# Feed-forward in-projections by seven block products in place of eight

## The reference, cut to what matters

```python
D_MODEL = 1024
D_FF = 2816
def swiglu(h, w_in_ff, w_out_ff):
    gu = h @ w_in_ff
    g, u = gu[..., :D_FF], gu[..., D_FF:]
    return (jax.nn.silu(g) * u) @ w_out_ff
def _ffn_sublayer(x, mod, j, nw_pre, nw_post, w_in_ff, w_out_ff):
    shift, scale, gate = _mod(mod, j)
    y = swiglu(_pre(x, nw_pre, shift, scale), w_in_ff, w_out_ff)
    return x + FFN_RES * gate * rmsnorm(y, nw_post)
```

## Time and profile before

| | us |
|---|---|
| median of 3 runs | 2815.43 |
| lowest, highest | 2812.68, 2815.85 |
| the profiled execution | 2815.84 |
| its span in the trace | 2814.1 |
| PE busy | 2647.8 (94%) |
| DVE busy | 1363.8 (48%) |
| ACT busy | 865.3 (31%) |
| POOL busy | 114.6 (4%) |

### The profile page before, as it was taken

The page is one execution under the profiler, slowest core; times in us unless marked ns, Lnnn a source line. Parts: engine busy times, 40 slices in busy tenths (PEclk is TensorE's granted clock), DMA queues, the critical chain, the costliest instruction groups (busy, mean ns, idle before and its releaser), DMA issues.

```text
span 2814.1 us, 33945 instructions
## 1 busy us (share of the span) xinstructions
PE 2647.8 (94%) x13880; PEld 2376.4 (84%) x13880; DVE 1363.8 (48%) x1871; ACT 865.3 (31%) x1145; POOL 114.6 (4%) x92
## 2 busy tenths in 40 slices
PE   5999999998977989999999999999998878799998
PEld 1999998887966789999988999999887656688887
DVE  2455456655455654544565533334455655522233
ACT  3211113443422451111344411113443433422232
POOL 0000000101200110000010100000101101000001
PEclk9999999999989999999999999999999999899999
DMA  6333334432200233333343333333432201322332
GB/s 228 128 119 120 140 135 164 152 119 79 79 1 1 97 121 120 119 136 140 135 164 123 125 125 137 126 127 120 135 120 80 79 1 60 135 90 97 106 111 75
DMA packets 84735, 314.25 MB, mean 112 GB/s; under 512 B 6944, under 2 KB 23328, under 8 KB 70944
## 3 DMA queue, kind: packets, MB, share of 16 engines
q1 hardware_dynamic: 77360, 297.20, 29.6%
q10 hardware_dynamic: 7280, 15.73, 1.7%
HBM read 310.81 MB, written 2.10 MB: 111 GB/s over the span
## 4 chain that ended last, share of the span: by engine, by line
PE 87%; DVE 7%; ACT 2%; issue 2%; DMA 1%; POOL 0%; SPq 0%; POOLq 0%; DVEq 0%; ACTq 0%
PE ps L1580 47%; PE ps L1594 25%; PE ps L795 5%; DVE w_lo L1319 2%; PE ps L1643 1%; PE ps L1653 1%; PE ps L885 1%; PE ps L901 1%; ACT w_hi L1104 1%; PE ps L876 1%; DVE arena L567 1%; PE ps L894 1%; PE ps L1627 1%; PE ps L895 1%; PE ps L822 1%
## 5 line engine op out<-in xcount | busy, mean ns | idle before, releaser
L1580 PE MATMUL ps<-xn_hi,w_hi 128*128 128x384 f32 (+2 forms) x2528 | 721.9, 340 | 21.8 <-DVE arena L1402 16.8
L1580 PE MATMUL ps<-xn_lo,w_hi 128*128 128x384 f32 (+2 forms) x2528 | 720.5, 340 | 0.0
L1580 PE MATMUL ps<-xn_hi,w_lo 128*128 128x384 f32 (+2 forms) x2528 | 720.3, 340 | 0.0
L1319 DVE TENSOR_TENSOR w_lo<-raw,w_hi 128x2048 fp32r<-128x2048 f32 x211 | 500.2, 2371 | 386.8 <-ACT w_hi L1104 386.6
L1580 PEld LDWEIGHTS ps<-xn_hi,w_hi 128*128 128x128 f32 x2528 | 464.7, 189 | 33.9 <-issue 17.3
L1104 ACT ACTIVATE w_hi<-raw 128x2048 fp32r<-128x2048 f32 x211 | 400.6, 1899 | 266.5 <-PE ps L1594 227.1
L1580 PEld LDWEIGHTS ps<-xn_lo,w_hi 128*128 128x128 f32 x2528 | 464.9, 189 | 11.1
L1580 PEld LDWEIGHTS ps<-xn_hi,w_lo 128*128 128x128 f32 x2528 | 464.5, 189 | 11.3
L1213 ACT ACTIVATE arena<-ps 128x384 f32 (+3 forms) x158 | 72.9, 497 | 1052.4 <-PE ps L1580 1052.4
L1338 DVE SCALAR_TENSOR_TENSOR junk<-acc,silu_row 128x1024 bf16<-128x1024 f32 x224 | 274.0, 1223 | 196.7 <-DMA acc<-w_ada_t 193.3
L1594 PE MATMUL ps<-w_hi,hj_hi 128*128 128x512 f32 x952 | 299.0, 395 | 23.1 <-DVE hj_lo L1327 10.2
(11 more groups left out here) (194 smaller groups left out, 2040.3 us busy)
## 6 DMA issues: line engine op xcount, KB each, us to landing
raw<-w_ff_in SPq DMA_DIRECT2D x104, 1024.0 KB, 5.4
raw<-w_ff_out SPq DMA_DIRECT2D x77, 1024.0 KB, 4.9
acc<-w_ada_t SPq DMA_DIRECT2D x128, 512.0 KB, 3.3
raw<-w_out SPq DMA_DIRECT2D x16, 1024.0 KB, 4.9
raw<-w_in SPq DMA_DIRECT2D x12, 1024.0 KB, 5.2
arena<-w_ada SPq DMA_DIRECT2D x4, 2048.0 KB, 18.7
gate_row<-norm_w ACTq DMA_DIRECT2D x12, 512.0 KB, 4.3
x<-x_in ACTq DMA_DIRECT2D x6, 512.0 KB, 6.8
```

The lines of the kernel that those rows point to most:

```text
L1319: nc.vector.tensor_tensor(w_lo[par][:, 0:width], raw[par][:, 0:width], w_hi[par][:, 0:width].bitcast(F32), ALU.subtract).then_inc(S["w_lo" ...
L1580: ins = mm(ps[:, 4 * b + part + c, col:col + wd], w[:, k, c, :], xx[:, k, t0:t0 + wd], start=(k == 0 and i == 0), stop=(k == KC - 1 and i ...
```

## The change

In stages (0,0), (0,2) and (1,0) the 18 full slots are computed by a form of Strassen's scheme. The left operand is the weights, cut in four: gate or up, and first or second half of the channels (a11, a12 gate, a21, a22 up, 512 columns each). The right one is x, cut by channel half and by token group. The slot's product of 2 x 2 blocks then takes seven block products of 12 matmuls (`product`, `fast_slot`). For it:

- the order of slots becomes lead, tail, then the 18 slots (also in the final stage, which is otherwise as before);
- the sums of x blocks (t) are made once a stage: POOL adds hi and lo of the first group again (`rebuild`, two ops of 1536 columns), DVE does six sums and four lo parts (`t_add`, `t_lo`, 1536 columns each), ACT four hi parts (`t_hi`). Two of the results lie where x does (`t13`), so x is stored to DRAM first in (0,2) and (1,0), and loaded again (from there, or from the input in (0,0)) at the start of the out-projection, six transfers of 512 KB each way;
- POOL makes the sums of weight blocks, four ops of 512 columns a slot (`sums`);
- splits of the weights are by pairs of blocks, 1024, 1024, 1024 and 512 columns (`pair_hi` on ACT, `pair_lo` on DVE), each when the products before have used the old ones;
- three products accumulate onto one already in a bank, after ACT has copied it out (`copy_out`, semaphore snap); DVE combines copies and banks (c11, c22, c12), and c22 must have read bank a before the seventh product goes to it;
- silu now runs on the copies, and DVE does two multiplies a slot;
- `gate_row` is scratch in these slots, so its load (`load_constants`) comes behind the last multiply;
- units go with all 18 slots in the three stages, none with the tail; (0,0) has twelve units in its out slots in place of eight.

The left-out new functions are short: `pair_hi`, `pair_lo`, `t_hi`, `t_add`, `t_lo`, `copy_out` are one instruction each with one wait before it, and ACT's part of the tail is its old part with `pair_hi` and `t_hi` between.

```diff
-ADA_TAIL = {(0, 0): (0, 13)}
-ADA_OUT = {(0, 0): (0, 14), (0, 2): (1, 7)}
+ADA_OUT = {(0, 0): (0, 13, 3), (0, 2): (1, 7, 2)}
 LEAD = 4
+ST = FC - LEAD
...
+        t13 = inner.enter_context(nc.sbuf_tensor("t13", [P, 2, 2, KC // 2, GW], F32R))
...
+        def pair_at(par0, i):
+            off = (0, 2 * HB, 0, 2 * HB)[i]
+            n = HB if i == 3 else 2 * HB
+            return [w_all[:, par0 if i < 2 else 1 - par0, a, off:off + n] for a in range(2)]
...
+        def fast_banks(s):
+            return (0, 1, 2) if s == 0 else (7, 5, 6)
...
+        def tail_steps(sub):
+            for k in range(LEAD, 2 * LEAD):
+                yield k, sub["slot"] + k, k - LEAD, k % 2
...
+        def fast_steps(sub, loop, per):
+            done = 0
+            for a, (l, h0, count) in enumerate(sub["ada_in"]):
+                last = a == len(sub["ada_in"]) - 1
+                trips = count - 1 if last else count
+                if trips:
+                    with loop(trips, per) as i:
+                        for s in range(2):
+                            yield i * 2 + (done + s), s, (l, i, h0, l * HALVES + h0)
+                done += 2 * trips
+            for s in range(2):
+                yield done + s, s, (l, count - 1, h0, l * HALVES + h0)
...
-                    load(n0 + LEAD, (par0 + LEAD) % 2, w_ff_in[l, j // 2, LEAD])
+                    due = {2 * LEAD + 2 * i + s: half for i, half in enumerate(halves) for s in range(2)}
+                    load(n0 + LEAD, (par0 + LEAD) % 2, w_ff_in[l, j // 2, 0])
                     for k in ahead:
                         if k + 1 in ahead:
-                            load(n0 + k + 1, (par0 + k + 1) % 2, w_ff_in[l, j // 2, (k + 1) % FC])
+                            load(n0 + k + 1, (par0 + k + 1) % 2, w_ff_in[l, j // 2, k + 1 - LEAD])
+                        if k == LEAD and sub["fast"] and sub["st"]:
+                            sp.wait_ge(S["xs"], sub["xn"])
+                            for t in range(NT):
+                                sp.dma_start(x_out[t], x[:, t, :]).then_inc(S["xs_out"], 16)
                         if k in due:
                             hl, h = due[k]
-                            for u in (2 * (k % 2), 2 * (k % 2) + 1) if k < FC else (k - FC,):
...
+                        if sub["fast"] and g == 0 and isinstance(s, int) and s == 1:
+                            sp.wait_ge(S["prod"], 6 * ST * (sub["st"] + 1) - 1)
+                            if sub["st"]:
+                                sp.wait_ge(S["xs_out"], 16 * NT * sub["st"])
+                            for t in range(NT):
+                                sp.dma_start(x[:, t, :], (x_out if sub["st"] else x_in)[t]).then_inc(S["x_back"], 16)
...
+            def rebuild(sub):
+                pool.wait_ge(S["xn_done"], sub["xn"])
+                for kh in range(2):
+                    hi, lo = x_block(kh, 0)
+                    nc.gpsimd.tensor_tensor(t_raw(kh), hi.bitcast(F32), lo.bitcast(F32), ALU.add).then_inc(S["t_x"], 1)
+            def sums(sub, q, par, first=False, second=False):
+                n, tq = q + (sub["slot"] + 2 * LEAD), q + ST * sub["st"]
+                a11, a12, a21, a22 = (raw[par][:, i * HB:(i + 1) * HB] for i in range(4))
+                s21 = s_sum(sub["slot"] % 2, first)
+                pool.wait_ge(S[f"w_raw{par}"], n * 8 + (16 - 8 * par))
+                if second:
+                    pool.wait_ge(S["w_used"], 2 * (sub["slot"] + 2 * LEAD) + START)
+                elif not first:
+                    pool.wait_ge(S["q_lo"], tq * 3 - 1)
+                adds.link(nc.gpsimd.tensor_tensor(s21[:, 1, :], a21, a22, ALU.add))
+                adds.mark(nc.gpsimd.tensor_tensor(a21, a11, a21, ALU.subtract))
+                nc.gpsimd.tensor_tensor(s21[:, 0, :], s21[:, 1, :], a11, ALU.subtract).then_inc(S["s_sum"], 1)
+                pool.wait_ge(S["s_sum"], tq * 2 + 1)
+                pool.wait_ge(S["q_lo"], tq * 3 + 1)
+                nc.gpsimd.tensor_tensor(a12, a12, s21[:, 0, :], ALU.subtract).then_inc(S["s_sum"], 1)
...
+                for q, s, half in fast_steps(sub, loop, 0):
+                    tq, n = q + st, q + n1
+                    a, d, b = fast_banks(s)
+                    r = (par0 + s + 1) % 2
+                    last = isinstance(q, int) and q == ST - 1
+                    act.wait_ge(S["prod"], tq * 6 + 1)
+                    copy_out(fast_tmp(2 * s), a)
+                    if not last:
+                        act.wait_ge(S[f"w_raw{r}"], (n + 1) * 8 + (16 - 8 * r))
+                        act.wait_ge(S["prod"], tq * 6 + 2)
+                        pair_hi(sub, 0, r)
+                    act.wait_ge(S["prod"], tq * 6 + 3)
+                    copy_out(fast_tmp(2 * s + 1), a)
+                    act.wait_ge(S["h_done"], n - n0 + sub["proj"])
+                    act.wait_ge(S["prod"], tq * 6 + 4)
+                    copy_out(p5, b)
+                    if not last:
+                        act.wait_ge(S["s_sum"], tq * 2 + 3)
+                        pair_hi(sub, 1, r)
+                    else:
+                        split_w(n + 1, par0)
+                    act.wait_ge(S["c11"], tq + 1)
+                    nc.scalar.activation(fast_tmp(2 * s), fast_tmp(2 * s), ACT.Silu).then_inc(S["silu11"], 1)
+                    act.wait_ge(S["prod"], tq * 6 + 6)
+                    if not last:
+                        act.wait_ge(S["s_sum"], tq * 2 + 4)
+                        pair_hi(sub, 2, r)
+                    else:
+                        first_out(sub)
+                    act.wait_ge(S["c12"], tq + 1)
+                    nc.scalar.activation(fast_tmp(2 * s + 1), fast_tmp(2 * s + 1), ACT.Silu).then_inc(S["silu"], 1)
+                    if not last:
+                        act.wait_ge(S["w_used"], n * 2 + 2 + START)
+                        pair_hi(sub, 3, r)
...
+                        if sub["fast"] and g == 0 and isinstance(s, int) and s == 0:
+                            act.wait_ge(S["h_done"], sub["proj"] + sub["in_slots"])
+                            load_constants(sub)
...
+                for k, n, f, s in tail_steps(sub):
+                    if k < 2 * LEAD - 1:
+                        split_w(n + 1, (par0 + s + 1) % 2)
+                    else:
+                        pair_lo(sub, 0, 0, par0)
+                        pair_lo(sub, 0, 1, par0, first=True)
+                    if k == LEAD:
+                        dve.wait_ge(S["t_x"], 2 * sub["st"] + 1)
+                        t_add(sub, 3, 0, t_raw(2), t_raw(0), ALU.subtract)
+                        t_add(sub, 4, 2, t_raw(3), t_raw(2), ALU.subtract)
+                    if k == LEAD + 1:
+                        dve.wait_ge(S["t_x"], 2 * sub["st"] + 2)
+                        t_add(sub, 5, 3, t_raw(3), t_raw(0), ALU.subtract)
+                        t_add(sub, 6, 1, t_raw(1), t_raw(3), ALU.subtract)
+                    if k == LEAD + 2:
+                        t_lo(sub, 2, 1)
+                    gate_mul(sub, k, f, s, (1,))
+                    if k == LEAD + 2:
+                        t_lo(sub, 1, 2)
+                    if k == LEAD + 3:
+                        t_lo(sub, 3, 3)
+                pair_lo(sub, 0, 2, par0)
+                pair_lo(sub, 0, 3, par0)
+                t_lo(sub, 4, 4)
+                for q, s, half in fast_steps(sub, own.loop, 0):
+                    tq, f, n = q + st, q + LEAD, q + n1
+                    a, d, b = fast_banks(s)
+                    r = (par0 + s + 1) % 2
+                    last = isinstance(q, int) and q == ST - 1
+                    hl, i, h0, g0 = half
+                    g_h, u_h = fast_tmp(2 * s), fast_tmp(2 * s + 1)
+                    dve.wait_ge(S["snap"], tq * 3 + 1)
+                    dve.wait_ge(S["prod"], tq * 6 + 2)
+                    nc.vector.tensor_tensor(g_h, g_h, ps[:, d, 0:GW], ALU.add).then_inc(S["c11"], 1)
+                    if not last:
+                        pair_lo(sub, q + 1, 0, r)
+                    unit(i + g0, i * 4 + (4 * g0 - 16 + 2 * s), 2 * s, streams(hl, h0))
+                    dve.wait_ge(S["snap"], tq * 3 + 3)
+                    dve.wait_ge(S["prod"], tq * 6 + 5)
+                    nc.vector.tensor_tensor(p5, p5, ps[:, a, 0:GW], ALU.add).then_inc(S["c22"], 1)
+                    if not last:
+                        pair_lo(sub, q + 1, 1, r)
+                    else:
+                        split_w(n + 1, par0)
+                    dve.wait_ge(S["prod"], tq * 6 + 6)
+                    nc.vector.tensor_tensor(u_h, u_h, ps[:, b, 0:GW], ALU.add).then_inc(S["c12"], 1)
+                    if not last:
+                        pair_lo(sub, q + 1, 2, r)
+                    else:
+                        first_out(sub)
+                    unit(i + g0, i * 4 + (4 * g0 - 15 + 2 * s), 2 * s + 1, streams(hl, h0))
+                    if s == 1:
+                        finish_units(i + g0, i + h0, i * 4 + (4 * g0 - 12))
```

(46 more changed lines are left out.)

205 lines of the change are left out of this document (148 added, 57 removed).

## The result

The changed kernel takes 2745.97 us (median of 4 runs, 2744.21 to 2750.59), the kernel before 2814.28 in the same comparison: a ratio of 0.976, 95% interval 0.9744 to 0.9775. The forecast was 2783; the gain is 68 us where 32.8 were forecast. On two other chips, where the kernel before took 2812.9 and 2815.2, the same kernel took 2761.4 and 2760.5, ratios of 0.9815 (0.9801 to 0.9828) and 0.9808 (0.9792 to 0.9824). So the gain is 68 us in the first comparison and 51 to 55 in two later ones, and both need a reason. (The chip of the first comparison is not known, and none of the later ones was measured twice, so what I put down to the chip could also be the occasion.)

The account below looks back on a forecast made before the run. TensorE, busy 94%, bounds the kernel before; in the new two-stream slots VectorE would. Gains 28.1 + 32.6, less 7.0, 19.9 and 1.0 (last stage's slot order), give 32.8 us off 2815.84: 2783 us, range 2734 to 2828.

Parts of the forecast that it names:

- The two-stream slot, walked: Slots whose units have two streams: VectorE, held up by GpSimd's sums, sets 15.9 us; 38 slots gain 28.1 us.
- What it removes: 54 in-projection slots: seven products of 12 matmuls for eight, 2.08 us less each, 14.56 left; ceiling 112.3 us.
- One-stream slots: 16 third-stage slots whose units have one stream: TensorE sets the pace at 14.6 us, gaining 32.6 us.
- The start: Start of each of three stages: first new slot's c22 comes late, 2.3 us each, 7.0 lost in all (0 to 18).
- The handover: Products to out-projection: TensorE idles for late out-weights, then runs at half clock; 19.9 us lost in all (0 to 28).
- Costed at nothing: Saving and reloading x, load_constants and the first stage's four extra units hide behind other work: 0 us.
- Free sums: Rival: GpSimd's sums fall into VectorE's waits and beside combines, all slots 14.6 us; 2733 us, chance 0.23.
- Lock without overlap: Rival: every GpSimd sum holds VectorE up in full, two-stream slots 17.0 us; 2824 us, chance 0.19.
- Clock: Rival: TensorE's clock falls after its idle time in each of 38 slots, 2.8 us each; 2889 us, chance 0.05.

Follow-up runs that it names:

- few sums: Changed kernel with a slot's four weight sums made over 8 of 512 columns from each stage's second slot on: 2718.39 us.
- the narrow stream: Changed kernel with the second stream of each modulation unit summed over 64 of its 1024 columns: 2713.64 us.
- the sums on VectorE: Changed kernel with the four weight sums of each slot from the second on made by VectorE, not GpSimd: 2729.29 us beside 2761.42 unedited.
- six sums: Changed kernel with the first and third weight sum of each slot made twice over: 2819.12 us.
- the early load: Changed kernel with the first out-projection weights' load issued ahead of the last slot's two units, not behind: 2742.36 us beside 2761.42 unedited.
- x not saved, first run: Changed kernel without the saves of x, which is reloaded from the input in all three stages; first of two runs: 2760.32 us.

## Why the prediction was right or wrong

**What fell: the size of one term, the two-stream slot.** The step *The two-stream slot, walked* said 15.9 us; it is 15.2 in the first comparison and 15.5 to 15.6 in the two later ones. So the gain on these slots, put at 28.1 us, was about 54 in the first comparison. The 2746 us lie inside the range of 2734 to 2828, but below the 2765 to 2800 that I thought likeliest. The mechanism is the one that it named: few sums, the narrow stream and the sums on VectorE each bring the pitch down to TensorE's or within 0.14 of it, and six sums raise it to 17.1. Three of its parts were too dear. It charged 1.26 us for each of four sums and let 1.0 us of them lie beside other work, 4.05 a slot; measured are 3.6 to 3.8. It took VectorE's own work at 11.4; by the same slot's records it is about 11.2. And it rounded the walk's 15.74 up for hops, which the slot in order of time does not show. Together that is 0.7 us a slot, about 25 us over 38 slots.

**The account of the rest**, from the profiled executions (2815.84 and 2745.93: 69.9 us). From the first new slot's start to the end of its last product the stages take 275.8, 276.8 and 264.3 us; the forecast was 288.5, 288.5 and 267.7. That is 27.8 us better, the slots' 25 among them. The handovers cost 8.7, 8.3 and 3.3 (the wait and the slow matmuls behind it) in place of 9.8, 9.8 and 7.4: 6.7 better. With the 32.8 of the forecast that gives 67.3, and 2.6 us are not placed.

- *What it removes*: right. 648 matmuls, and 14.56 us a slot wherever TensorE sets the pace.
- *One-stream slots*: right, 14.6 forecast, 14.56 measured.
- *The start*: near. The first c22 of each stage is about 3.0 us late where 2.3 were taken.
- *The handover*: right in its chain and in the clock of the first two stages; the early load took 19.1 us back. The third was too dear: TensorE idled 2.97 us, and its clock stayed at 1.00. That it stayed was luck: in the two later profiles of the same kernel the wait was 3.16 and 3.07 us, and in another run even 2.83, and the clock was at 0.50 behind each.
- *Costed at nothing*: right for the saves (without them the kernel took 1.8 us less, inside the spread). The reload was not tried by itself.
- *Free sums* was wrong in its mechanism, though its time, 2733, lay nearer to 2746 than mine (on the later chips, 2761, mine was the nearer). Only the profile and the experiments tell the two apart.
- *Lock without overlap* was wrong: sums do run beside the combines.
- *Clock*: wrong for this kernel, whose waits for c22 are 1.7 us at most, but not far off. With six sums the waits reached 4 us and the clock fell inside the loop, in the first stage about once in two slots. The argument against this rival was one gap of 1.70 us. The trace of before holds better evidence: in its mixer (783 to 916 us) TensorE waits again and again for 2.3 to 2.5 us, and its clock falls to 0.50 six times.

**What the forecast left out.** The walk let the second unit wait for its rows, but didn't say that this makes the slot depend on how fast a chip's transfers are. The kernel before doesn't show it, because VectorE idles half of the time there and waits 3.46 us for rows at no cost.

## What to carry to other kernels

When matmuls are traded for elementwise sums, add up the engine that also needs the SBUF: a sum that GpSimd makes cost VectorE 0.91 us here, one that VectorE made itself 0.60 to 0.69, so the same work was dearer to VectorE on the idle engine than on its own. Once VectorE sets the pace, a transfer issued when its buffer comes free is part of the loop, and a few tenths of a microsecond of a chip's transfers turned into 9 us here; put independent work between the release of the buffer and its next use. And compare an edit with an unedited kernel on the same chip, since here the chip moved the time by 15 us, nearly as much as the early load did.

## What the runs showed of the hardware

- GpSimd's 512-column add takes 1.28 to 1.30 us alone, and holds a step of VectorE with two SBUF inputs up by 0.6 to 1.1 us, 0.91 for each sum on average; even VectorE's bias add over 8 columns (0.17 us alone) takes 0.97 to 1.19 beside one. The holding is mutual: GpSimd's fourth sum takes 2.21 us where it waits for VectorE.
- The length of a single wait did not tell what TensorE's granted clock would do. At the third handover it stayed at 1.00 behind 2.97 us (first comparison), and was at 0.50 behind 2.83 (x not saved, first run), 2.88 (sums on VectorE), 2.89 (second stream narrow) and 3.07 and 3.16 (the later profiles of the unedited kernel). In the six-sum run it fell behind waits of 2.84, 2.85 and 3.15 us and stayed at 1.00 behind 2.88 and 2.91. In the mixer of before it fell behind some waits of 2.31 us and not behind others of 2.31 and 2.50. Behind each of the longer waits at the handovers, 3.2 to 6.3 us, it was at 0.50.
- Transfers differ from chip to chip (or occasion): in the new slots of the first stage a 1 MB weight load landed after a median of 5.4 us in the first comparison and 5.7 and 5.8 in the later ones, while the kernel before, bound by TensorE, took the same time within 0.1% on all.
